# A two-block fp32 transformer kernel: its ring of weight loads goes from seven buffers to five, its ring of split weights from four to five

## The reference

```python
mod  = silu(c)     @ w_mod + b_mod        # [2048] @ [2048, 12288]: six shifts, scales and gates
cmod = silu(c_ctx) @ w_mod + b_mod
p_lat = modulate(rmsnorm(x, g_pre_mix),   sh1,  sc1)  @ w_in
p_ctx = modulate(rmsnorm(ctx, g_pre_mix), csh1, csc1) @ w_in
m_lat = mlstm_group(p_lat, p_ctx, ...)    # chunked mLSTM, 8 heads
d_lat = diff_group(p_lat, p_ctx, ...)     # differential attention, 8 heads
y_lat = concat([m_lat, d_lat]) @ w_out
x = x + ga1 * rmsnorm(y_lat, g_post_mix)
h = modulate(rmsnorm(x, g_pre_ffn), sh2, sc2)
x = x + ga2 * rmsnorm(conv_ffn(h, w_up, conv_w, conv_b, w_down), g_post_ffn)
```

## Time and profile before

| | |
|---|---|
| three runs | 3010.19, 3012.24, 3014.29 us; median 3012.24 |
| the profiled execution | 3010.53 us, of which the trace spans 3008.7 |
| busy | PE 2878.0 us (96%), weight loads of PE 2349.9, DVE 2046.6 (68%), ACT 1243.9 (41%), POOL 144.7 (5%) |
| granted clock of TensorE | 0.986 of full speed over the span |
| traffic of the weights and the rest | 589.44 MB, 196 GB/s on average |

### The profile page before, as it was taken

The page is one execution under the profiler, slowest core; times in us unless marked ns, Lnnn a source line. Parts: engine busy times, 40 slices in busy tenths (PEclk is TensorE's granted clock), DMA queues, the critical chain, the costliest instruction groups (busy, mean ns, idle before and its releaser), DMA issues. The chain is left out here.

```text
span 3008.7 us, 38123 instructions
## 1 busy us (share of the span) xinstructions
PE 2878.0 (96%) x14307; PEld 2349.9 (78%) x14307; DVE 2046.6 (68%) x2904; ACT 1243.9 (41%) x2122; POOL 144.7 (5%) x225
## 2 busy tenths in 40 slices
PE   6999999998999999999999999998989999999997
PEld 2587667988778888788787888887878888887786
DVE  3368645837778889997895768774765756775455
ACT  3322535417454555454444332324444224445353
POOL 1100000001010000000001000000001001001000
PEclk9999999998999999999999999999999999999999
DMA  9877045841858778787785646662423544684333
GB/s 359 305 265 246 17 136 158 283 153 35 297 197 268 246 257 255 239 269 256 262 305 173 189 148 175 217 216 64 142 93 131 197 152 150 205 280 125 100 140 131
DMA packets 282967, 589.44 MB, mean 196 GB/s; under 512 B 31090, under 2 KB 64090, under 8 KB 279201
## 3 DMA queue, kind: packets, MB, share of 16 engines
q1 hardware_dynamic: 272384, 546.64, 55.4%
q0 software_dynamic: 10000, 39.72, 3.8%
q10 hardware_dynamic: 400, 0.66, 0.1%
HBM read 572.21 MB, written 14.72 MB: 195 GB/s over the span
## 5 line engine op out<-in xcount | busy, mean ns | idle before, releaser
L3137 DVE TENSOR_TENSOR w_lo<-raw,w_hi 128x1024 fp32r<-128x1024 f32 (+2 forms) x668 | 785.6, 1188 | 384.1 <-ACT w_hi L3108 375.0
L3108 ACT ACTIVATE w_hi<-raw 128x1024 fp32r<-128x1024 f32 (+2 forms) x668 | 677.8, 1031 | 879.9 <-PE bank L3200 630.9
L732 DVE SCALAR_TENSOR_TENSOR acc<-raw,sc_t,acc 128x1024 f32<-128x1024 f32 x480 | 601.8, 1281 | 44.1 <-DMA acc<-in_b_ada 25.1
L3198 PE MATMUL bank<-w_hi,l_hT_hi 128*128 128x512 f32 (+1 forms) x1056 | 390.5, 370 | 10.3 <-DVE w_lo L3137 9.3
L3200 PE MATMUL bank<-w_hi,l_hT_lo 128*128 128x512 f32 (+1 forms) x1056 | 386.9, 366 | 0.0
L3199 PE MATMUL bank<-w_lo,l_hT_hi 128*128 128x512 f32 (+1 forms) x1056 | 386.8, 366 | 0.0
L3198 PE MATMUL bank<-w_hi,f_hT_hi 128*128 128x512 f32 x704 | 278.2, 395 | 1.7 <-DVE mod L780 1.1
L3200 PE MATMUL bank<-w_hi,f_hT_lo 128*128 128x512 f32 x704 | 274.9, 390 | 0.0
L3199 PE MATMUL bank<-w_lo,f_hT_hi 128*128 128x512 f32 x704 | 274.8, 390 | 0.0
L3198 PEld LDWEIGHTS bank<-w_hi,l_hT_hi 128*128 128x128 f32 x1056 | 198.3, 188 | 51.4 <-DVE w_lo L3137 13.1
L3200 PEld LDWEIGHTS bank<-w_hi,l_hT_lo 128*128 128x128 f32 x1056 | 198.2, 188 | 31.5
(11 more groups left out here) (471 smaller groups left out, 4633.2 us busy)
## 6 DMA issues: line engine op xcount, KB each, us to landing
raw<-in_w_in SPq DMA_DIRECT2D x240, 512.0 KB, 4.8
raw<-in_w_mod SPq DMA_DIRECT2D x192, 512.0 KB, 5.5
raw<-in_w_ada SPq DMA_DIRECT2D x192, 512.0 KB, 4.7
raw<-in_w_up SPq DMA_DIRECT2D x176, 512.0 KB, 4.8
raw<-in_w_out SPq DMA_DIRECT2D x96, 512.0 KB, 4.8
raw<-in_w_down SPq DMA_DIRECT2D x88, 512.0 KB, 5.6
raw<-in_w_in SPq DMA_DIRECT2D x32, 288.0 KB, 3.4
raw<-in_w_ukv SPq DMA_DIRECT2D x32, 256.0 KB, 3.4
```

The costliest lines, as they stand in the source:

```text
L732: e.scalar_tensor_tensor(acc[a][:, :], raw[s % RAW_SLOTS][:, :], scalar, acc[a][:, :], ALU.mult, ALU.add).then_inc(fma_done, 1)
L3108: e.activation(slot(w_hi[u % SPLIT_SLOTS], g.width), slot(raw[s % RAW_SLOTS], g.width), ACT.Copy).then_inc(hi_ready, 1)
L3137: e.tensor_tensor(slot(w_lo[u % SPLIT_SLOTS], g.width), slot(raw[s % RAW_SLOTS], g.width), slot(w_hi[u % SPLIT_SLOTS], g.width).bitcast(F3 ...
L3198: e.matmul(o, xh[:, k, tok], hi[:, kk, :], start=first, stop=False)
```

## The change

The ring of loads gets five buffers and not seven, the ring of split units five pairs and not four. Both take 15 buffers of 4 KB a partition, so `acc1` and all else stay where they are. The call for the mLSTM stage of block 1, whose `fill` was the size of the split ring, now says 4 outright, so the same four units are split ahead of its barrier as before.

```diff
@@ -30,8 +30,8 @@
 UNIT_K = 2
 UNIT_W = 512
 FMA_W = 1024
-RAW_SLOTS = 7
-SPLIT_SLOTS = 4
+RAW_SLOTS = 5
+SPLIT_SLOTS = 5
@@ -2262,7 +2262,7 @@
-        stage(fill=SPLIT_SLOTS, pe=m_pe, act=m_act, pool=m_pool, dve=m_dve)
+        stage(fill=4, pe=m_pe, act=m_act, pool=m_pool, dve=m_dve)
```

## The result

The changed kernel takes **3029.39 us** (median of 4 runs, 3028.02 to 3029.94) against 3012.15 us before: 17.2 us slower, a ratio of 1.0056 (95% interval 1.0039 to 1.0074). The forecast was 3017.4 us, and 3029.39 is above its range of 3010 to 3026. The trace spans 3027.5 us, 18.8 more than before.

A forecast was written before the change was run, and what follows sets the result against it. PE, busy for 96% of the span, was taken as the bound. Front +5.2, `w_out` stage 0, other places +0.3 and fifth split pair -0.3 sum to +5.2 us on 3012.24: 3017.4 us, range 3010 to 3026.

The forecast's parts named there:

- The bound, and the split ring: Whole span: PE bounds, busy 96%; a fifth split pair could return at most 30.3 us of `w_lo` waits, taken as -0.3.
- The -0.3 us at 2939.28: PE's 0.29 us wait there was laid to the full ring of four split pairs; the fifth pair returns 0.3 us.
- The front, the mechanism: Before 140 us: five buffers hold one turn; SP's next turn waits for PE's first M load; lateness adds up to 5.2 us.
- the term of +5.2 us: Front: four late turns, 3.8 us latency each and 1.35 us between landings, make the unbroken `w_in` 5.2 us late.
- The w_out stage of block 1: Fewer loads could bring the gate vector 2.7 us earlier or weight loads 2.7 us later; taken as 0.
- Elsewhere: All places but the front and block 1's `w_out` stage: two load buffers fewer cost +0.3 us, between 0 and +3.
- The signs that it named: Changed profile: `w_mod` waits about 15 us, SP's wait well beyond 84.3, `w_lo` waits near 30, ACT's waits little fewer.
- The argument from those 312: ACT's 312 waits for PE, 630.9 us in all, were read as showing the loads' lead over PE mostly whole.
- the three signs of being wrong: `w_lo` stalls down 10 us or more; front over by 136 us; new `w_lo` waits after 140 us beside late loads.
- The rival that all is hidden: Front: loads land sooner or existing waits absorb PE's lateness; costs 0 to 2.5 us, time about 3013.5; chance 0.2.
- The rival of a larger loss: Three DVE-bound stretches lose 2.7 us each, 3025.5 us in all; front gaps may lower PE's clock, 1.8 us; chance 0.2.
- The page's formula: Any 512 KB load: fixed 2.0 us plus bytes at 436 GB/s, 3.2 us; the front would then lose 2.8 us.

The follow-up runs named there:

- e1: Five load buffers and four split pairs, the two buffers left over idle, against the kernel before: 3029.65 us, ratio 1.0048.
- e9: Seven load buffers and four split pairs up to load 314 (830 us), then five and five, against the kernel before: 3010.99 us, ratio 0.9992.
- e4: Five load buffers and five split pairs in the front (up to load 84), then seven and four, against the kernel before: 3023.34 us, ratio 1.0031.
- e11: Four load buffers and four split pairs throughout, against the kernel before: 3092.59 us, ratio 1.0264.
- e5: The changed kernel run again on another chip, against the kernel before: 3028.98 us, ratio 1.0055.

## Why the prediction was wrong, point by point

- **The bound, and the split ring.** Right that PE bounds, and that a fifth pair returns next to nothing: e1 and the change are alike, e9 doesn't differ from before. The -0.3 us at 2939.28 was misread. In all later traces PE waits there too, 0.2 to 2.3 us: 1.85 after the change, 1.94 in e1, 1.77 in e9. What comes late ahead of ACT's split is an evacuation on DVE that waits for the last normalisation's vector, `fin_g`, not a buffer.
- **The front, the mechanism.** Right: SP frees a turn with PE's first M load of the turn before, and each turn adds. e4 shows it alone at 9 to 10 us.
- **The front, the size.** The step that failed first is the term of +5.2 us: four turns, each with one load of 3.8 us and 1.35 us "between landings that follow one another". Every turn cost more. At load 21 PE was 2.5 us late already (51.85 against 49.33), where the sum had 1.0, and 2.6 at load 23, where it had 1.2: load 21 wasn't alone in the queue, and landed 5.5 us after its issue at 46.35. From the issue at 69.05 to the use of load 40 at 80.08 are 11.0 us where the sum had 3.8 + 5.4 = 9.2; from 98.39 to ACT's load 53 at 105.93 are 7.5, not 3.8 + 2.7 = 6.5, and the same place one turn later, 133.62 to 141.37, took 7.75. Those are 1.4, 1.8, 1.0 and 1.25 us more. The spacing itself held for most landings, as 77.42, 78.74 and 80.08 for loads 38 to 40 show; but near the head of each burst (the loads that SP issues once a buffer comes free) one came late. Load 38 landed 3.0 us behind load 37, 53 came 2.4 behind 52, and 72 2.3 behind 71. The kernel before has the same (load 55 is 2.3 us behind 54), so it could have been read ahead. Against this total of 5.45 stand 2.0 us that PE got back between loads 23 and 36, 1.6 of them because the kernel before, and not the changed one, ran that stretch at half the clock: 5.2 + 5.45 - 2.0 = 8.65, and 8.6 was measured at 143.83. That it isn't over 10 us there is luck of that one execution. The fall of the clock at 144 us (1.6 us) was named and priced (1.8) in a rival but left out of the sum, and so was that the trace before had one of its own, which the earlier trace rows showed.
- **The w_out stage of block 1.** The step "A turn is then 3.8 of latency and 2.3 of splitting, 6.1 us, against 5 x 1.35 = 6.75" was wrong. It used the latency of a lone load at a place where loads come at the full rate; with five under way it was 5.8 us, the round 8.1, and the stage lost 4.4 us that I had taken as 0 between -2.7 and +2.7. The gate vector didn't come earlier either: DVE waited 10.03 us for it, where it had waited 8.07.
- **Elsewhere.** +0.3 taken, and e9 shows none. Five buffers are enough where the weights are asked for more slowly. The densest such stretch is in the `w_down` stage; the trace before moved 312 GB/s there at its height. Its window after the change:

```profile
1400.00:1500.00 100.00, 100.00 (x444) 81.67 (x444) 82.59 (x72) 40.44 (x41) 0.00 (x0) 1.00 0.91 313
```

  PE is busy there without a gap at 313 GB/s, just what the ring of five gave above. So five buffers are only just enough there, and with four (e11) this stage lost 24 us.
- **The sum.** 10.2 + 4.4 = 14.6 by the trace of the change, 3012.15 + 14.6 = 3026.8; measured 3029.4, and on another chip (e5) 16.6 us over the kernel before by the ratio. The missing 2 to 3 us are no more than what single executions differ by: the front alone by up to 5 us. The averages over the traces above come to 11.8 + 4.8 = 16.6.
- **The signs that it named.** Waits for M loads went to 13.1 us (15 was said), SP's wait for PE to 95.9 us (well beyond 84.3 was said), and the `w_lo` waits stayed near 30. That ACT's wait for PE would fall in number by little was wrong: 312 became 78. The argument from those 312, that the lead of the loads is mostly whole, doesn't hold for the changed kernel; but e9 shows that behind load 314 PE lost nothing by it. One of the three signs of being wrong came: new waits for `w_lo` beside late loads after 140 us, six of them in the `w_out` stage.
- **The rival that all is hidden** was right that loads land sooner with fewer under way (6.9 us became 5.8 in the `w_out` stage), and wrong in that this hides the loss: a load with nothing ahead of it still took 3.6 to 4.1 us.
- **The rival of a larger loss** named the right side and nearly the size (3025.5) but another cause. The stretches where DVE is the bound, such as the one from 1817 us, didn't lose.
- **The page's formula.** The prediction set 3.2 us a load by the Trainium skill (DMA: Bandwidth & Descriptors, Anatomy of one DMA) against 3.65 in the rows and followed the rows. Both were of a load by itself; the measured 5.5 to 6.9 us with four to seven in the ring were what counted.

## What to carry to other kernels

A ring of loads delivers at most its bytes divided by one round of a buffer, and the round must be taken with the latency that loads have when the ring is full at that place, not with that of a lone load: the earlier trace rows had 4.8 and the busy stages 5.5 to 6.9, where 3.65 was the shorter of the two that I used. The latency itself falls with the depth, so a trace of the deeper ring gives two limits: with 3.8 us five buffers come to 430 GB/s, with the 6.9 of that stage to 286, and 314 was measured. The stage took 363 with seven, so most of what lies between these limits is a loss, and no loss wasn't the middle. Look for the stages that ask for nearly the full transfer rate; only in those two, the front and the `w_out` stage, did two buffers less cost anything that these runs can tell. And where a buffer is freed by the engine at the end of the chain, in program order, count how many loads of the pattern the ring holds: here, at exactly one turn, each turn of the front handed its lateness on to the next. Before the difference of two traces is put down to the change, look at the granted clock in both, and at more than one execution.

## What the runs showed of the hardware that wasn't expected

Behind an empty ring a burst of loads doesn't keep the spacing of a full queue: 11.0 us for five loads from the issue of the first, where 3.8 and four times 1.35 are 9.2. Most followed one another in 1.3 us, but one near the head of each burst came 2.3 to 3.0 us behind the one before it, while the DMA engines weren't idle (0.97 of the time and 354 GB/s over 74.4 to 77.4 us). With fewer loads under way the DMA engines also moved less for the time that they were busy: 363 GB/s at a share of 1.01, 337 at 0.95, 314 at 0.93 and 262 at 0.80 come to 359, 355, 338 and 328 GB/s at a share of 1. A stop of PE for a late unit costs more than the wait that the rows name: 4.4 us for 2.4 us of waits in the `w_out` stage. And after 2.7 us of waits at 143 us over 3 us of matmuls ran at half the clock, which cost 1.6 us more. It isn't so each time: e1 has waits of 2.00 and 0.32 us at the same place and no fall.
